# Layer step: x in four pieces, first factors among the gate chunks, keys turned ahead, marks for four experts, residual rows summed by TensorE

## The reference

```python
proj = x @ w_in                        # 1024 -> 6144 channels, and 16 more (b_raw, a_raw)
qkv_raw, z, b_raw, a_raw, lx, ly = jnp.split(proj, [...], axis=-1)
q, k, v = silu(causal_dwconv(qkv_raw))
q = l2norm(q) * 128 ** -0.5            # t * rsqrt(sum(t * t) + 1e-6), per head of 128
k = l2norm(k)
beta, g = sigmoid(b_raw), -exp(a_log) * softplus(a_raw + dt_bias)
o, s_new = gdn_chunked(q, k, v, beta, g, s0)     # decay, triangular solve, states
lru_out = rg_lru(lx) * gelu(ly)
h1 = layer_norm(ALPHA * x + concat(rms_norm(o) * silu(z), lru_out) @ w_out)
idx, gw = route(h1)                    # 8 of 64 experts for each token
ffn = shared_swiglu(h1) + sum(gw[:, j] * expert[idx[:, j]](h1) for j in range(8))
y = layer_norm(ALPHA * h1 + ffn)
```

## Time and profile before

| | |
|---|---|
| median of 3 runs | 1485.98 us (1485.22 to 1489.07) |
| the profiled execution | 1485.28 us |
| its span in the profile | 1483.5 us |
| mean granted clock of TensorE | 0.989 of full |
| TensorE busy | 1427.5 us, 96% |
| VectorE busy | 975.6 us, 66% |
| ScalarE busy | 621.7 us, 42% |
| GpSimd busy | 353.3 us, 24% |
| DMA | 313.27 MB, mean 211 GB/s |

### The profile page before, as it was taken

How to read it: one execution, slowest core, us unless ns; L and a number is a source line. 1 busy time by engine, 2 the same in 40 slices (tenths; PEclk the granted TensorE clock), 3 DMA queues, 4 the chain that set the end, 5 groups by cost and what they waited for, 6 DMA issues and landing times. The chain is left out here.

```text
span 1483.5 us, 21149 instructions
## 1 busy us (share of the span) xinstructions
PE 1427.5 (96%) x8131; PEld 1137.5 (77%) x8135; DVE 975.6 (66%) x1765; ACT 621.7 (42%) x967; POOL 353.3 (24%) x235
## 2 busy tenths in 40 slices
PE   7999999998999999999898999999999999999967
PEld 5999999997998887788766667667767766766723
DVE  5648877517576775056977767767767776776538
ACT  3566333324424423010134555555565565555400
POOL 0000000004243330003443333333333333333200
PEclk9999999998999999999999999999999999999988
DMA  5222222210000003600749999999999999999667
GB/s 210 72 71 86 86 85 85 85 59 1 2 1 12 20 1 137 271 29 5 284 165 359 356 368 369 374 374 366 373 369 365 367 370 365 366 368 369 233 282 288
DMA packets 55641, 313.27 MB, mean 211 GB/s; under 512 B 15168, under 2 KB 16192, under 8 KB 36096
## 3 DMA queue, kind: packets, MB, share of 16 engines
q1 hardware_dynamic: 35792, 276.19, 49.3%
q0 software_dynamic: 19760, 35.89, 6.5%
HBM read 301.37 MB, written 42.12 MB: 232 GB/s over the span
## 5 line engine op out<-in xcount | busy, mean ns | idle before, releaser
L2217 POOL DMA_INDIRECT expert_rows<-lru,slot_ids x64 | 154.3, 2411 | 304.5 <-DVE lru L2436 286.5
L320 PE MATMUL bank<-x_hi,w_hi 128*128 128x274 f32 x768 | 223.9, 291 | 0.0
L322 PE MATMUL bank<-x_hi,w_lo 128*128 128x274 f32 x768 | 222.9, 290 | 0.0
L321 PE MATMUL bank<-x_lo,w_hi 128*128 128x274 f32 x768 | 221.9, 289 | 0.0
L2429 DVE TENSOR_TENSOR gate_up_lo<-wide,gate_up_hi 128x2048 fp32r<-128x2048 f32 x84 | 192.1, 2286 | 40.3 <-ACT gate_up_hi L2369 40.3
L2296 PE MATMUL bank<-gate_up_hi,rows_hi 128*128 128x512 f32 x512 | 206.4, 403 | 0.0
L2297 PE MATMUL bank<-gate_up_lo,rows_hi 128*128 128x512 f32 x512 | 200.4, 391 | 0.0
L2298 PE MATMUL bank<-gate_up_hi,rows_lo 128*128 128x512 f32 x512 | 199.9, 390 | 0.0
L2369 ACT ACTIVATE gate_up_hi<-wide 128x2048 fp32r<-128x2048 f32 x84 | 161.1, 1919 | 0.0
L320 PEld LDWEIGHTS bank<-x_hi,w_hi 128*128 128x128 f32 x768 | 144.9, 189 | 0.8 <-issue 0.5
L321 PEld LDWEIGHTS bank<-x_lo,w_hi 128*128 128x128 f32 x768 | 145.0, 189 | 0.3
(11 more groups left out here) (348 smaller groups left out, 2575.1 us busy)
## 6 DMA issues: line engine op xcount, KB each, us to landing
wide<-in_w_exp SPq DMA_DIRECT2D x43, 2048.0 KB, 14.7
kept_wide<-in_w_exp SPq DMA_DIRECT2D x21, 2048.0 KB, 14.5
w_out_first<-in_w_in SPq DMA_DIRECT2D x48, 512.0 KB, 3.5
wide<-in_w_exp SPq DMA_DIRECT2D x22, 1024.0 KB, 13.0
w_out_first<-in_w_exp SPq DMA_DIRECT2D x21, 1024.0 KB, 13.2
kept_rows<-in_w_exp SPq DMA_DIRECT2D x21, 1024.0 KB, 13.2
expert_rows<-expert_rows SPq DMA_DIRECT2D x5, 1536.0 KB, 20.5
wide<-in_w_out SPq DMA_DIRECT2D x5, 1024.0 KB, 10.0
```

What stands on the lines that cost most here:

```text
L320: nc.tensor.matmul(out, wh[:, k, :], x_hi[:, k, at], start=(k == 0), stop=False)
L321: nc.tensor.matmul(out, wh[:, k, :], x_lo[:, k, at], start=False, stop=False)
L322: last = nc.tensor.matmul(out, wl[:, k, :], x_hi[:, k, at], start=False, stop=(k == DC - 1))
L2217: return pool.indirect_dma_start(out=dram["expert_rows"], out_offset=bass.IndirectOffsetOnAxis(ap=index, axis=0), in_=source, in_offset=No ...
```

## The change

**x.** The queue now brings `w_ba`, a quarter of x (two blocks), the first `w_in`, then the other three quarters. ScalarE and VectorE split the first weights behind the second block of x instead of ahead of the first.

**First factors.** Squares, sums, roots and factors move into a class `RowFactors`. For tile 0 and the sample tile they are made in the projection stage, among the last eight chunks, which are now written out (the loop has three rounds). In chunk 43 one sum of tile 0 follows each group of three matmuls, in chunk 45 one sum of the sample tile; each is one column wide. The latter go into the same bank as the former, so the first of them waits until VectorE has read the prompt's sums. ScalarE squares behind chunks 40 and 42, takes the exponential behind 41 and the roots behind 45 and 46. The sums of tiles 1 to 3 stay 112 wide and in the delta stage.

**Delta.** The first scaled values are made by VectorE in two operations instead of by ScalarE in eight. In every tile the keys are turned before `k_state` of the tile before, and at the end values and keys of the sample tile before `k_state` of the last tile. GpSimd scales the sample's decay with the keys' factor (`scale_decay_few`), and VectorE multiplies once instead of twice.

**Experts.** FIRST = 4: one more expert is marked and summed ahead; its rows are gathered behind the last slot write, once the rows of expert 0 have been turned, and before the slot ids are loaded. The marks now lie over the space of the layer norm's weights.

**Combine.** The residual rows of four of the five tiles are copied into PSUM by TensorE (`begin_sum`, two matmuls each), three of them behind the last expert and one at the start of the combine stage; a prompt tile's first five rows are added on top. The sample tile's layer norm reads PSUM. For the first three prompt tiles VectorE adds rows 6 and 7 to row 5 and then PSUM to that.

```diff
+class RowFactors:
...
+    def square(self, act, t, squares):
+        _, at, w, _, _ = token_tiles()[t]
+        if self.turn(t):
+            act.wait_ge(self.summed, self.turn(t))
+        qkv = self.mem.carve(self.mem.qkv, 0, NQ, TW)
+        self.nc.scalar.activation(squares[:, :, 0:w], qkv[:, 0:2 * H, at:at + w], ACT.Square).then_inc(self.squared, 1)
+    def sum_one(self, pe, t, squares, j, n):
+        w = token_tiles()[t][2]
+        if j == 0:
+        last = self.nc.tensor.matmul(self.mem.bank[6][0:w, j:j + n], squares[:, j, 0:w], self.mem.consts("ones")[:, 0:n],
+                                     start=True, stop=True)
+        if j == 2 * H - 1:
+            last.then_inc(self.summed, 1)
+    def read(self, dve, t):
+        w = token_tiles()[t][2]
+        dve.wait_ge(self.summed, self.turn(t) + 1)
+        self.nc.vector.tensor_scalar(self.norm_a[0:w], self.mem.bank[6][0:w, 0:2 * H], 1e-6, None, ALU.add)\
+            .then_inc(self.read_, 1)
+    def root(self, act, t):
+        w = token_tiles()[t][2]
+        act.wait_ge(self.read_, self.turn(t) + 1)
+        self.nc.scalar.activation(self.norm_b[0:w], self.norm_a[0:w], ACT.Sqrt).then_inc(self.rooted, 1)
+    def make(self, dve, steps, t):
+        nc, w, i = self.nc, token_tiles()[t][2], self.set_of(t)
+        norm, row, ks, kd, qs = (f[i][0:w] for f in (self.norm, self.row, self.ks, self.kd, self.qs))
+        dve.wait_ge(self.rooted, self.turn(t) + 1)
+        inverse_root(nc, steps, norm, self.norm_a[0:w], self.norm_b[0:w], self.norm_c[0:w])
+        rk, rq = norm[:, H:2 * H], norm[:, 0:H]
+        steps.done(nc.vector.tensor_scalar(rq, rq, P ** -0.5, None, ALU.mult))
+        steps.done(nc.vector.tensor_tensor(row, rk, self.beta[0:w, t, :], ALU.mult))
+        steps.done(nc.vector.tensor_tensor(kd, rk, self.egd[0:w, t, :], ALU.mult)).wait()
+        steps.link(nc.vector.tensor_tensor(ks, row, self.eg[0:w, t, :], ALU.mult))
+        nc.vector.tensor_scalar(ks, ks, -1.0, None, ALU.mult)
+        nc.vector.tensor_tensor(qs, rq, self.eg[0:w, t, :], ALU.mult).then_inc(self.ready, 1)
...
-            load(0, 0, True)
             sp.dma_start(w_ba, dram["w_ba"]).then_inc(s_wba, 16)
-            for half in range(2):
-                ks = slice(4 * half, 4 * half + 4)
-                sp.dma_start(x_t[:, ks, :], dram["x_t"][:, ks, :]).then_inc(s_x[half], 16)
+            for i in range(4):
+                ks = slice(2 * i, 2 * i + 2)
+                sp.dma_start(x_t[:, ks, :], dram["x_t"][:, ks, :]).then_inc(s_x[i], 16)
+                if i == 0:
+                    load(0, 0, True)
...
+                    channels = last
+                    if between:
+                        between(DC * half + k)
                 if isinstance(n, int) and n == 0 and half == 0:
...
-                if k % 4 == 0:
-                    pe.wait_ge(s_x[k // 4], 16)
+                if k % 2 == 0:
+                    pe.wait_ge(s_x[k // 2], 16)
...
                     project_gates(pe, n - 3)
-            with pe.Fori(2, 6) as u:
+            def sum_prompt(at):
+                rf.sum_one(pe, 0, squares[0], at, 1)
+            def sum_sample(at):
+                if at == 0:
+                    pe.wait_ge(rf.read_, 1)
+                rf.sum_one(pe, TILES, squares[1], at, 1)
+            with pe.Fori(2, 5) as u:
                 for j in range(8):
                     project(pe, u * 8 + j, j)
+            for j in range(8):
+                project(pe, 40 + j, j, between={3: sum_prompt, 5: sum_sample}.get(j))
...
-            split(0)
             for k in range(DC):
-                act.wait_ge(s_x[k // 4], 16)
+                if k == 2:
+                    split(0)
+                act.wait_ge(s_x[k // 2], 16)
...
+                if j == 0:
+                    act.wait_ge(s_fin, 24)
+                    rf.square(act, 0, squares[0])
+                elif j == 1:
+                    act.wait_ge(s_left, 1)
+                    nc.scalar.activation(egd, egd, ACT.Exp).then_inc(s_egd, 1)
+                elif j == 2:
+                    rf.square(act, TILES, squares[1])
+                elif j == 5:
+                    rf.root(act, 0)
+                elif j == 6:
+                    rf.root(act, TILES)
...
                     lru_output(b)
             for n in range(40, NCH):
                 split(n + 2)
+                if n == 40:
+                    dve.wait_ge(s_gread, 1)
+                    nc.vector.tensor_tensor(egd, gtot, gsum, ALU.subtract).then_inc(s_left, 1)
+                elif n == 44:
+                    rf.read(dve, 0)
+                elif n == 45:
+                    dve.wait_ge(s_egd, 1)
+                    rf.make(dve, steps, 0)
+                elif n == 46:
+                    rf.read(dve, TILES)
+                    rf.make(dve, steps, TILES)
...
                 transposed(t, 2, key_banks(t), s_vt)
+                transposed(t, 1, query_banks(t), s_kt)
                 if t:
                     k_state(t - 1)
-                transposed(t, 1, query_banks(t), s_kt)
-                if not t:
-                    sums(0)
-                    sums(TILES)
...
                         update(t - 1)
-            k_state(TILES - 1)
             transposed(TILES, 2, key_banks(TILES), s_vt)
             transposed(TILES, 1, query_banks(TILES), s_kt)
+            k_state(TILES - 1)
...
-                dve.wait_ge(s_et, 2 * turn(TILES) + 2)
-                steps.link(nc.vector.tensor_tensor(out[0:DEC], few(7, part), decay[0:DEC, :, 0:DEC], ALU.mult))
-                factor = norm[factor_set(TILES)][0:DEC, H:2 * H].unsqueeze(2).to_broadcast([DEC, H, DEC])
-                nc.vector.tensor_tensor(out[0:DEC], out[0:DEC], factor, ALU.mult).then_inc(done, 2)
+                dve.wait_ge(s_few_decay, 1)
+                nc.vector.tensor_tensor(out[0:DEC], few(7, part), decay[0:DEC, :, 0:DEC], ALU.mult).then_inc(done, 2)
...
-            dve.wait_ge(s_egd, 1)
-            read_sums(0)
-            factors(0)
-            read_sums(TILES)
+            for g, hs in groups:
+                dve.wait_ge(s_vt, g + 1)
+                nc.vector.tensor_tensor(v_beta[0][:, hs, :], in_bank(key_banks(0) + g, P, P),
+                                        beta[:, 0, hs].unsqueeze(2).to_broadcast([P, 4, P]), ALU.mult).then_inc(s_vb, 1)
             nc.vector.memset(state[0], 0.0)
-            factors(TILES)
...
+FIRST = ROWS + 1
+SUMS_AHEAD = (1, 0, 3)
...
+def begin_sum(pe, nc, mem, n):
+    w = combine_order()[n][2]
+    pe.wait_ge(mem.sums_begun[n], 16)
+    for c in range(2):
+        last = nc.tensor.matmul(mem.bank[2 * (n % 4) + c][0:w, :], mem.consts("ident")[0:w, 0:w],
+                                mem.sums[n][0:w, 512 * c:512 * c + 512], start=True, stop=False)
+    last.then_inc(mem.sums_copied, 1)
...
-            for e in range(ROWS):
+            for e in range(FIRST):
...
+        pool.wait_ge(rows_turned, 2)
+        read_tokens(pool, dram, mem.rows[0], first_ids[:, ROWS:FIRST]).then_inc(mem.rows_gathered[0], 16)
         pool.wait_ge(s_listed, 16 * TOPK * (TILES + 1))
         pool.dma_start(mem.ids[:, :], dram["slots"].rearrange("(c p e) w -> c p (e w)", p=P, e=NE)[0])\
...
-        for b in range(ROWS, 2 * ROWS):
+        for b in range(FIRST, 2 * ROWS):
...
+        for n in SUMS_AHEAD:
+            begin_sum(pe, nc, mem, n)
...
-        by_tensor = (8, 6, 6, 6, 5)
-        pieces = ((0, 8), (0, 1, 3, 6, 8), (0, 3, 6, 8), (0, 3, 6, 8), tuple(range(TOPK + 1)))
+        by_tensor = (8, 5, 5, 5, 5)
+        pieces = ((0, 8), (0, 1, 3, 5, 8), (0, 3, 5, 8), (0, 3, 5, 8), tuple(range(TOPK + 1)))
...
+            begin_sum(pe, nc, mem, 2)
...
-                                                start=(j == 0), stop=(j == by_tensor[n] - 1))
+                                                start=(n == last_n and j == 0), stop=(j == by_tensor[n] - 1))
...
+                    wait_piece(dve, n, first)
+                    for j in range(first + 1, TOPK):
+                        add_row(j, rows[0:w, first, :])
                 dve.wait_ge(s_sum, n + 1)
+                if n == 0:
+                    for c in range(2):
+                        last = nc.vector.bn_stats(st[:, 6 * c:6 * c + 6], sums[c])
+                    steps.link(last)
+                    nc.vector.bn_aggr(st[:, 12:14], st[:, 0:12]).then_inc(s_var, 1)
...
+                    for c in range(2):
+                        last = nc.vector.scalar_tensor_tensor(a[:, at[c]], sums[c], st[:, 12:13], ln[0:w, 0, at[c]],
+                                                              ALU.subtract, ALU.mult)
+                    last.then_inc(s_read, 1)
+                else:
+                    for c in range(2):
+                        last = nc.vector.tensor_tensor(a[:, at[c]], (a if final else rows[0:w, first, :])[:, at[c]], sums[c],
+                                                       ALU.add)
+                    last.then_inc(s_read, 1)
```

192 lines of the change are left out of this document (89 added, 103 removed).

## The result

The changed kernel takes 1478.59 us in the median of 4 runs (1478.14 to 1479.62); the kernel before, with one more run beside it, 1487.53 (1485.22 to 1489.71). The ratio is 0.9941 with a 95% interval of 0.9922 to 0.9960. The sign was right; 1466 was not reached, nor the range up to 1474. The profiled execution has a span of 1476.4 us against 1483.5, so 7.1 us are to be explained from the traces. The kernel before runs less evenly than the changed one: measured again beside the experiments, its medians were 1484.7 to 1489.7. So steps of a few us are read from landmarks inside the traces first, and the medians stand beside them.

What follows compares the result with a forecast made beforehand. TensorE, busy 96% of the span, bounds the kernel with its work and waits. Terms -3.5, -3.9, -3.9, +0.2, -6.0, -3.0, +0.3 sum to -19.8: from 1485.28 to 1465.5, median 0.7 above, 1466 us; range 1458 to 1474.

Steps and rivals of the forecast that it cites:

- x in four pieces: Kernel start: first matmuls begin earlier on a quarter of x, -3.5 us (ends -1.8 and -4.2).
- the arrival of the second quarter: Load of x at the start: second quarter lands at 9.65 us, after a TensorE wait of 0.5 us.
- The prompt's sums: Projection, chunk 43: 16 sums of two 128-column records between matmuls add 3.5 us.
- The sample's sums: Projection, chunk 45: 16 narrow 32-column sums between matmuls add 2.3 us (ends 1.2 and 3.5).
- The wait: Projection, chunk 45: TensorE stands still 2.8 us until VectorE has read the prompt's sums.
- the upper end of the projection: Projection stage: +8.6 us in sum, from 5 to 12, the upper end with a slow spell after the stop.
- Rival A: Projection: stop lowers clock, sums uncover loads, 3.4 us more; delta start gains 1.8 less; 1471 us, chance 0.13.
- against it: here dense matmuls stand on both sides: Chunk 45: argument against half clock following the stop, as it did a 2.53 us wait before.
- Start of the delta stage: Delta stage up to level 1: applied 15.5 us after the stage's start, -12.5 us (ends -10.7 and -13.7).
- Keys, marks and gather, combine: Delta, expert and last stages: keys -3.9, marks +0.2, gather -6.0, combine -3.0, early copies +0.3 us.
- Rival B: Expert stage: slot ids come about 8 us later, most of the 6.0 is lost; 1471 us, chance 0.08.
- Rival D: Expert loop: weights don't land earlier, 0.5 us wait in each of 60 rounds; 1496 us, chance 0.03.

Runs made afterwards that it cites:

- e1: Changed kernel with the sample tile's sums in a PSUM bank of their own, so without the wait in chunk 45: 1468.61 us.
- e5: Changed kernel with the edits of e1 and e4 together: 1464.43 us.
- e4: Changed kernel with VectorE's first inverse of the sample tile moved to just before the sample's own next step: 1475.39 us.
- e6: e5 with the sample's sums 128 columns wide: 1462.77 us.
- e2: Changed kernel with the wait kept in chunk 45 and the sample's sums moved to chunk 46: 1473.57 us, a single execution.
- e9: e5 with the sample's sums in one block behind chunk 45, the prompt's still one by one in chunk 43: 1461.18 us.
- e10: e9 with the edit of the keys undone, so turned in the order of before: 1464.34 us.
- e11: e9 with the fourth expert neither marked nor gathered ahead, three as before: 1468.81 us.
- e12: e9 with the combine stage of before, without residual copies into PSUM: 1466.36 us.

## Why the prediction was wrong, step by step

**x in four pieces: direction right, size off.** -3.5 forecast with ends -1.8 and -4.2, -5.4 measured. The step that failed is the arrival of the second quarter, put at 9.65 because the same bytes were ahead. The bytes were the same, but in smaller pieces and another order they moved at 379 and 409 GB/s instead of 227 and 263, and the wait of 0.5 us did not come. That is only half of the miss. The other half is luck: with x as in the changed kernel the first matmul began at 5.2 to 5.5 in every profile, but the records became short 3.2 us later in the changed kernel, 4.0 in e1 and e5, 5.8 in e4, and the split products began at 14.30, 14.87, 14.67 and 15.55 (15.80 in e6). So the step is worth 4 to 5.4. With 5.3 us, as before, they would begin near 15.3, an estimate from e4 and from 0.46 against 0.22 us for each record: -4.4, and 1.0 us more by the time at which the records became short.

**The prompt's sums: right.** 3.5 forecast; chunks 43 and 44 take 15.8 us together instead of 12.2, so 3.6.

**The sample's sums: a term mis-sized.** 2.3 forecast, at most 3.5; 5.6 measured (16 x 0.35 in e1, which is also what its projection is longer by than before, less the prompt's 3.6). I took the record of a block (0.037 us) and one uncovered load for an operation that stands alone between loads of another width. No row of before had that, and the nearest, the two 40-column products, had 128-column loads.

**The wait: right in its length, wrong in what follows.** The stop is 2.7 of 2.8 us. Behind it came 7.8 us of slow clock (e1 against the changed kernel: 10.5 by landmarks, less the stop), where the upper end of the projection, 12, left about 2 for it. Rival A named this mechanism and took the same 2, with no row beside it. e2 shows that 2 is right when dense matmuls follow: some 4 us of half clock, 1.8 us lost. The step that failed is thus "against it: here dense matmuls stand on both sides": the change itself had put narrow sums among them.

3.6 + 5.6 + 2.7 + 7.8 = 19.7: the whole of the projection's step.

**Start of the delta stage: right to level 1, and not followed further.** Level 1 was applied 15.9 us after the stage's start, forecast 15.5; VectorE's products began 6.3 us after it, forecast 6.1. But the chain was costed only as far as the next landmark. Pulling the start together pushed GpSimd's mask products and a small VectorE operation on top of one another, and 4.4 us went back within the next level (e4). The trace of before had the same thing to show. Timelines of VectorE and GpSimd, 330 to 372 us:

```profile
342.28 4.31 DVE L139 TENSOR_SCALAR factors<-factors 32x16 f32<-32x16 f32 x1
```

```profile
342.82 3.74 POOL L1180 TENSOR_TENSOR kept_rows<-delta_consts,factors 128x1024 f32<-128x1024 f32 x2
```

A small operation of VectorE, whose neighbours of the same size take 0.16 us, lasts 4.31 us and ends with GpSimd's two mask products, at 346.6.

**Keys, marks and gather, combine: right.** -3.7 (forecast -3.9), -6.3 with the marks (-5.8), -3.0 with the border (-2.7). Undone one at a time in e9 they cost 3.2, 7.6 and 5.2 us by the medians (e10, e11, e12) and 4.1, 5.7 and 4.0 by the traces. The combine stage is thus worth 1 to 2 us more in e9 than the changed kernel's landmarks say; the runs of e9 and of e12 each spread over about 2 us. Rival B did not come: the slot ids are there at 785.9, and ScalarE waits 0.7 us for them in all. Rival D did not come either: expert rounds stay at 10.0 us.

Put together the steps differ from the forecast by -1.9, +11.1, -0.3, +4.4, +0.2, -0.5 and -0.3, in all 12.7 us: 1466 + 12.7 = 1478.7. The range was too narrow because its upper end for the projection left 2 us for a slow spell that cost 7.8 and 3.5 for sums that cost 5.6, and because nothing stood in it for the time behind level 1.

## What to carry to other kernels

A wait like this one, 2.7 us in a full TensorE stream, is to be charged with its length and with the slow clock behind it, and how long that lasts depends on what follows: dense matmuls brought the clock back after some 4 us, a stream with narrow one-column sums among its matmuls did not for 20. How 128-column sums do behind a wait no run tells. So take such waits out first (here a second PSUM bank was enough), and put small helper matmuls between large ones in the width of their neighbours, or, if they are narrow, in one short block. When a chain is shortened, follow it one step past the landmark that you costed, on every engine, and look for what now meets.
